# The second output piece of each state-space turn as a high and a low half, and VectorE's low halves placed behind the decayed scores

## What is computed

```python
h = rms_norm(x, mix_pre_g[i])
proj = h @ w_in[i]
...
xbc = jax.nn.silu(causal_depthwise_conv(xbc, conv_w, conv_b))
y = ssd_chunked(xs, dt, a, bm, cm, d_skip)          # 8 groups
y = y * jax.nn.silu(z.astype(f32))
yg = y.reshape(bsz, seqlen, N_GROUPS, D_INNER // N_GROUPS)
yg = yg * lax.rsqrt(jnp.mean(yg * yg, axis=-1, keepdims=True) + RMS_EPS)
y = (yg.reshape(bsz, seqlen, D_INNER) * norm_g.astype(f32)).astype(z.dtype)
return y @ out_w
...
mixed = (g_conv * conv_out + g_ssm * ssm_out) @ w_out[i]
```

## Time and profile before

| | |
|---|---|
| median of 3 runs | 910.43 us (910.02 to 910.46) |
| profiled execution, its own time | 910.08 us |
| its span, first to last instruction | 908.0 us |
| TensorE busy | 899.3 us (99%) |
| VectorE busy | 736.6 us (81%) |
| ScalarE busy | 580.8 us (64%) |
| granted TensorE clock | 0.999 of full speed |

### The profile page before, as it was taken

How to read it: one execution, slowest core, us unless ns; L and a number is a source line. 1 busy time by engine, 2 the same in 40 slices (tenths; PEclk the granted TensorE clock), 3 DMA queues, 4 the chain that set the end, 5 groups by cost and what they waited for, 6 DMA issues and landing times.

```text
span 908.0 us, 18312 instructions
## 1 busy us (share of the span) xinstructions
PE 899.3 (99%) x6623; PEld 847.7 (93%) x6623; DVE 736.6 (81%) x1361; ACT 580.8 (64%) x998; POOL 38.0 (4%) x50
## 2 busy tenths in 40 slices
PE   9999999999999999999999999999999999999997
PEld 7999999999999999998888888999999999999886
DVE  5999898888989988689888646889979988888533
ACT  5649878797877575566666535679656755666332
POOL 1000111111110000000000000100000000000000
PEclk9999999999999999999999999999999999999999
DMA  9577588877875647456555555445447455555601
GB/s 335 181 267 231 143 199 236 248 219 218 241 203 192 209 166 247 145 161 236 196 186 185 193 187 170 147 171 189 143 134 257 158 192 185 182 179 175 228 1 47
DMA packets 48510, 172.04 MB, mean 189 GB/s; under 512 B 5668, under 2 KB 6344, under 8 KB 48328
## 3 DMA queue, kind: packets, MB, share of 16 engines
q1 hardware_dynamic: 43488, 154.74, 51.2%
q0 software_dynamic: 2880, 10.49, 6.1%
q10 hardware_dynamic: 2088, 6.08, 1.8%
HBM read 159.72 MB, written 1.09 MB: 177 GB/s over the span
## 4 chain that ended last, share of the span: by engine, by line
PE 66%; issue 24%; DVE 6%; ACT 2%; DMA 1%; POOL 1%; SPq 0%; POOLq 0%; ACTq 0%; DVEq 0%
PE A L472 10%; PE A L473 10%; PE A L474 10%; PE B L696 5%; PE A L504 4%; PE B L504 3%; PE B L472 2%; PE B L473 2%; PE B L474 2%; PE A L506 2%; DVE w_lo L1397 2%; PE B L506 2%; PE B L777 2%; PE A L777 1%; PE A L485 1%
## 5 line engine op out<-in xcount | busy, mean ns | idle before, releaser
L1397 DVE TENSOR_TENSOR w_lo<-raw,w_hi 128x1024 fp32r<-128x1024 f32 x249 | 301.8, 1220 | 72.7 <-ACT w_hi L930 72.1
L930 ACT ACTIVATE w_hi<-raw 128x1024 fp32r<-128x1024 f32 x249 | 259.4, 1051 | 74.6 <-PE A L778 20.9
L472 PE MATMUL A<-h,w_hi 128*128 128x256 f32 x952 | 274.5, 288 | 0.2 <-DVE sc L2017 0.2
L474 PE MATMUL A<-h,w_lo 128*128 128x256 f32 x952 | 269.2, 283 | 0.0
L473 PE MATMUL A<-h,w_hi 128*128 128x256 f32 x952 | 269.2, 283 | 0.0
L472 PEld LDWEIGHTS A<-h,w_hi 128*128 128x128 f32 x952 | 182.1, 191 | 3.3 <-issue 2.6
L473 PEld LDWEIGHTS A<-h,w_hi 128*128 128x128 f32 x952 | 182.3, 191 | 0.3
L474 PEld LDWEIGHTS A<-h,w_lo 128*128 128x128 f32 x952 | 182.2, 191 | 0.0
L472 PE MATMUL B<-h,w_hi 128*128 128x256 f32 x352 | 100.1, 284 | 0.0
L473 PE MATMUL B<-h,w_hi 128*128 128x256 f32 x352 | 99.6, 283 | 0.0
L474 PE MATMUL B<-h,w_lo 128*128 128x256 f32 x352 | 99.6, 283 | 0.0
(11 more groups left out here) (313 smaller groups left out, 1635.0 us busy)
## 6 DMA issues: line engine op xcount, KB each, us to landing
raw<-in_weights_dram SPq DMA_DIRECT2D x289, 512.0 KB, 4.3
w_lo<-raw POOLq DMA_DIRECT2D x20, 512.0 KB, 4.8
csrow<-cs_dram ACTq DMA_DIRECT2D x9, 512.0 KB, 4.9
x<-in_x_dram SPq DMA_DIRECT2D x4, 256.0 KB, 5.3
bd<-in_lru_w_dram ACTq DMA_DIRECT2D x1, 1024.0 KB, 5.7
out_dram<-m_wide SPq DMA_DIRECT2D x3, 256.0 KB, 2.1
raw<-in_weights_dram SPq DMA_DIRECT2D x2, 256.0 KB, 4.8
par<-in_params_dram SPq DMA_DIRECT2D x1, 379.0 KB, 6.3
```

Of the source, the lines that this page charges most:

```text
L472: mm(dst, wh, lo, start=first, stop=False, skip_group_check=free)
L474: return mm(dst, wl, hi, start=False, stop=last, skip_group_check=free)
L930: F(w_hi[:, s, :], raw[:, s, :], ACT.Copy).then_inc(hi_ready, 1)
L1397: V.tensor_tensor(w_lo[:, s, :], raw[:, s, :], w_hi[:, s, :].bitcast(F32), ALU.subtract).then_inc(lo_ready, 1)
```

## The change

The second out piece (number 6) of turns 1 to 6 and of turn 7 leaves `NATIVE` and becomes a split piece. Its operand `yn[:, 1]` is cut too: ScalarE makes `yn_hi` (`y_high`, behind `silu_bc`), VectorE `yn_lo` (`y_low`, behind the decayed scores and one low half). The new tiles share memory with `stage` and `stage2`. ScalarE converts one more piece a turn (`split(0)`). VectorE's list in the loop becomes 6, 7, 0', 1', 3', 4', 5', no entry is taken before the scores, and one is taken behind `decayed_scores`, two behind `y_gated`, two ahead of `y_mean`, and two ahead of `y_normed`. In turn 7, where none of the pieces ahead is in `LOW`, the list before is 7, 8, ... 13 and then 6, 7, ... 13; it is taken at the same places, except that `y_mean` comes ahead of the entries that in the loop precede it.

```diff
-NATIVE = frozenset(GLU_NATIVE) | frozenset([LOOP0 + 8 * i + n for i in range(GROUPS - 1) for n in OUT_AT]) | frozenset(range(TAIL0, PW0))
+NATIVE = frozenset(GLU_NATIVE) | frozenset([LOOP0 + 8 * i + OUT_AT[0] for i in range(GROUPS - 1)]) | frozenset(range(TAIL0, PW0))
...
             def out_piece(p, turn, g, c, between=None):
-                native_loaded(p, turn)
-                pe.wait_ge(scale_read, g + 2)
+                split = p not in NATIVE
+                if split:
+                    split_ready(p, turn)
+                    pe.wait_ge(yn_low, g + 1)
+                else:
+                    native_loaded(p, turn)
+                    pe.wait_ge(scale_read, g + 2)
                 for m in range(KD):
                     if between is not None and m == KD // 2:
                         y_transposes(between)
+                    if split:
+                        ins = tile(p % RING, m, yn_hi[:, c, :], yn_lo[:, c, :], acc_out(m), False, False, True)
+                        continue
...
+            def y_high(g, cs=(1,)):
+
+                act.wait_ge(scale_read, g + 2)
+                for c in cs:
+                    ins = F(yn_hi[:, c, :], yn[:, c, :], ACT.Copy)
+                ins.then_inc(yn_high, 1)
...
+                split(0)
                 split(1)
                 split(2)
                 silu_bc(g)
+                y_high(g - 1)
                 drain_input(0, 0, base + IN_AT[0], t)
...
-            for n in range(3):
-                split_hi(GATES0 + n + LEAD)
+            split_hi(GATES0 + LEAD)
             silu_bc(g)
+            split_hi(GATES0 + 1 + LEAD)
+            y_high(g - 1)
+            split_hi(GATES0 + 2 + LEAD)
...
+            def y_low(g, cs=(1,)):
+
+                dve.wait_ge(yn_high, g + 1)
+                for c in cs:
+                    ins = V.tensor_tensor(yn_lo[:, c, :], yn[:, c, :], yn_hi[:, c, :].bitcast(F32), ALU.subtract)
+                ins.then_inc(yn_low, 1)
...
                 if first:
                     conv_inputs(g, (0, 1))
+                    conv_inputs(g, (2, 3))
+                else:
                     lo()
-                    conv_inputs(g, (2, 3))
-                lo()
                 looped = more and first
...
                 x_by_dt(g)
                 decayed_scores(g)
                 lo()
+                if first:
+                    y_low(g - 1)
...
                 y_gated(g)
-                lo(1 if first else 2)
+                lo(2)
...
                 if looped:
-                    lo()
+                    lo(2)
                     y_mean(g)
                 else:
                     y_mean(g)
-                    lo()
+                    lo(2 if first else 1)
...
-                lo()
+                lo(2 if first else 1)
                 y_normed(g, read)
                 lo(len(los))
```

More of the change, by code:

```diff
@@ L131, in split_order @@
 def split_order(p, turn=0):
-    return sum(q not in NATIVE and q not in LOW for q in range(p)) + 1 + (6 - len(LOW_AT) if p < GATES0 else 8) * turn
+    return sum(q not in NATIVE and q not in LOW for q in range(p)) + 1 + (7 - len(LOW_AT) if p < GATES0 else 8) * turn
 def low_turn(p):
@@ L190, in hybrid_kernel @@
         scale = sb("scale", [P, TT])
+        s0 = ExitStack()
+        yn_hi = sb("yn_hi", [P, 2, T], F32R, s0)
+        yn_lo = sb("yn_lo", [P, 2, T], F32R, s0)
+        s0.close()
         stage = sb("stage", [P, 2, T])
@@ L351, in hybrid_kernel @@
         yt_ready, first_tap = sem("yt_ready"), sem("first_tap")
+        yn_high, yn_low = sem("yn_high"), sem("yn_low")
         conv_operand_ready, mixed_ready = sem("conv_operand_ready"), sem("mixed_ready")
@@ L688, in y_scale, with split_ready @@
                 spread_scale(g + 2)
-            def out_piece(p, turn, g, c, between=None):
-                native_loaded(p, turn)
-                pe.wait_ge(scale_read, g + 2)
+            def split_ready(p, turn):
+                if p in LOW:
+                    pe.wait_ge(low_added[(p - LOOP0) % RING], 16 * low_turn(p) + 16 * turn)
+                else:
+                    pe.wait_ge(lo_ready, split_order(p, turn))
+            def out_piece(p, turn, g, c, between=None):
+                split = p not in NATIVE
[5 more added lines that the diff above has]
+                    pe.wait_ge(scale_read, g + 2)
                 for m in range(KD):
@@ L1674, in group_turn @@
                     conv_inputs(g, (0, 1))
-                    lo()
-                    conv_inputs(g, (2, 3))
-                lo()
+                    conv_inputs(g, (2, 3))
+                else:
+                    lo()
                 looped = more and first
```

## The result

The changed kernel takes 918.99 us (median of 4 runs, 918.55 to 919.55) against 910.22 us before in the same session (909.78 to 910.46): the ratio is 1.0099, 95% interval 1.0086 to 1.0112, 8.8 us slower. The forecast was 6.0 slower, within 912.0 to 919.5. The profiled execution took 919.55 us with a span of 917.4.

A forecast was written before the change was run, and what follows sets the result against it. TensorE, busy 899.3 of 908.0 us, was taken to bound the kernel; the loop's +2.6 and the gates turn's +3.4 made +6.0, so 916.4 us, range 912.0 to 919.5. Offsets count from d, the start of VectorE's decayed scores.

The forecast's parts named there:

- The new wait: TensorE waits 0.94 us for POOL's scale each loop turn; y_mean at d + 12.24, y_scale at d + 13.54.
- nothing in the change touches that part of the path: TensorE's stretch from y_scale to the next turn's d stays 14.42 us, making the loop turn 27.96 us.
- ScalarE in some turns: ScalarE's unbroken chain, 17.81 grown to 19.07 us, decides some loop turns, with next d at 27.5, 28.3 or 28.9.
- The floor for the loop without it: Six loop turns of at least 27.96 us, 167.8 us against 166.00, +1.8 us.
- The gates turn, +3.4: Turn after the loop: VectorE's memset for the convolution's sums comes 3.73 us later, less 0.33, so +3.4 us.
- the expected wait of 2 us at the convolution's sums: In the gates turn TensorE arrives only 1.47 us later and waits about 2 us at the sums on ones.
- The slack of 0.33 us: Gates turn: time from the end of VectorE's memset to TensorE's sums, subtracted from the 3.73 us shift.
- Loads at nothing: SP's load queue was costed at nothing; the change should remove ScalarE's late load of 222.01.
- the saving to come through: Rival A: TensorE's 4.0 us shorter line makes the kernel faster; chance 0.06 of a time below 908.6.

The follow-up runs named there:

- experiment 1: Changed kernel with y_mean moved ahead of its last taps in the loop, the low half of 3' behind add_parts: 915.46 us, ratio 1.0064.
- experiment 10: Changed kernel with a fourth matmul, low by low, in every second tile of the split out pieces: 919.09 us, ratio 1.0098.
- experiment 8: Changed kernel with TensorE's loop over six turns written out, other engines keeping theirs: 917.55 us, ratio 1.0084.
- experiment 9: Kernel before the change with TensorE's loop written out, as a control: 910.30 us, ratio 1.0004.
- experiment 4: Changed kernel with y_high and the conversions of 6 and 0' behind decays on ScalarE in the loop: 919.39 us, ratio 1.0108.
- experiment 6: Changed kernel with y_mean ahead of its last taps and three ScalarE steps behind the exponentials, both in the loop: 915.68 us, ratio 1.0065.
- experiment 7: The kernel of experiment 6, plus two low halves ahead of the scores in the gates turn: 913.09 us, ratio 1.0036.
- experiment 11: The kernel of experiment 7 with TensorE's loop written out as well: 915.34 us, ratio 1.0057.
- experiment 12: Changed kernel with y_mean early, the gates turn's low halves ahead, and only y_high moved behind ScalarE's exponentials: 912.20 us, ratio 1.0023.
- experiment 5: Kernel before the change, both out pieces native, no y_high or y_low, only VectorE's low halves placed as in the change: 913.31 us, ratio 1.0035.
- experiment 3: Changed kernel with, in the gates turn alone, two low halves ahead of the scores, one behind y_gated, one behind y_mean: 916.42 us, ratio 1.0073.

## Why the prediction was right

The direction, the place and the mechanism in the loop were right, and the size was 2.8 us short. Part of that closeness is luck. The sum had 0.8 us for ScalarE that did not come and was 0.7 us short in the gates turn; these two nearly cancel, and what remains is one missing term of 2.8 us.

- *The new wait.* `y_mean` at d + 12.34 and `y_scale` at d + 13.52 stand within 0.1 us of the forecast, and experiments 1 and 10 show that this wait decides the turn: without it 3.4 us of the six turns go, and lengthening TensorE's own line up to it costs nothing.
- *The step that was mis-sized: "nothing in the change touches that part of the path", 14.42 us from `y_scale` to d.* It measured 14.88. `y_scale` is the last work of TensorE's loop. When the scale is there 1.3 us or more ahead of TensorE, the jump back costs nothing; when TensorE waits for it, or it comes only 0.06 us ahead (experiment 1), the jump lies open. Experiments 8 and 9 show that it is the loop: written out, it costs 0.06 instead of 0.46 us after the same wait, and nothing changes in the kernel before. That is 0.46 us in each of six turns, 2.8 us against the forecast. Against the kernel before it is 2.1, since 14.42 was the shortest of its six turns and their mean is 14.54. That queued matmuls hide the jump fits all of this; no run shows the queue itself.
- *ScalarE in some turns (+0.8 of the +2.6).* It did not decide (experiment 4); the squares started at d + 8.8 to 9.05, not 9.2 and 9.8. The floor for the loop without it, +1.8, and 2.8 for the jump make 4.6; the trace has 4.67. As the next limit it was placed rightly: experiment 1 meets it at 27.93 us a turn, between the 27.5 and 28.3 that its chain gave. The prediction calls that chain unbroken; it holds one pause of 0.64 to 0.67 us a turn, before and after the change alike, so the 19.07 us came out at 19.06.
- *The gates turn, +3.4.* VectorE's terms were right to 0.03 us. POOL's time was not: 2.73 us beside two low halves, where I had kept 1.59. That and the halved clock moved the end of the delay from VectorE's memset to TensorE: 4.11 instead of 3.4, a wait of 3.39 us for the scale instead of about 2, and the expected wait of 2 us at the convolution's sums did not appear. The slack of 0.33 us that the forecast took off was also too large, as half of it is the step from the memset's end to the sums' start.
- *Loads at nothing.* Right in the changed kernel: no load is waited for between the squares and the exponentials any more, as at 222.01 before. In experiments 6, 7 and 11, where ScalarE's steps stand later, loads become the limit.

The forecast's chance of 0.06 for the saving to come through stood on a low price of VectorE's work. No version reached it: the nearest, experiment 12, is 0.23% slower than before.

## What to carry to other kernels

An engine at 99% is not the only one without room: before time is taken from it, measure for each partner how long its unbroken chain is between two meeting points, and how many tenths are left. Work put on a partner is free only in its idle time, and then it matters on which side of the release it stands; here the same low half was free ahead of the scores and cost a wait behind them. A result that is needed at the end of a hardware loop costs more than its wait when it comes late or only just in time, and a small operation that another engine waits for should not start beside long ones.

## What the runs showed of the hardware

- TensorE, from the start of two transposes at the end of a loop's body to the next matmul: 0.13 us when what they need was there 1.3 us ahead or more (the kernel before, experiment 5), in the turns that jump back 0.57 to 0.63 us after waits of 0.35 to 0.96 us and also without a wait when it was there only 0.06 us ahead (experiment 1), 0.19 us after a wait of 0.80 in straight code (experiment 8). The way to the next d was the same 14.9 us after waits of 0.35 and 0.96.
- POOL's power of 128x2 numbers took 0.87 to 0.99 us beside VectorE's taps (128x256), 1.59 to 1.66 beside one low half (128x1024), 2.73 beside two. The Trainium skill (SBUF — State Buffer, SBUF: two separate sides) says that a VectorE operation with two SBUF inputs and a GpSimd operation that reads SBUF hold a shared port pair exclusively, each for its whole instruction. Steps of 0.7 and then 1.1 us, with a low half at 1.13 us in sequence, fit that, and the taps, which also have two SBUF inputs but last 0.4 us, cost far less. No run shows the port itself.
- The granted clock of TensorE fell to about half, the level of 1.2 GHz for most or all of the stretch, after waits of 3.39 and 3.40 us (0.56 for 3.9 us in the changed kernel, 0.50 for 4.2 us in experiment 1), and after one of 3.15 us (0.59 for 4.2 us in experiment 10), and stayed at 1.00 after 2.74 us in experiment 5 and 1.11 us in experiment 3. In experiment 11, with waits of 0.42 to 1.49 us in the four turns before, it fell to 0.69 for 5.5 us after a wait of only 1.83 us, so the last wait alone does not tell.
